# A hybrid decoder step: the fifth value products placed ahead of the first transposed outputs

## The reference

```python
x = half_ffn(x, ...)                                  # x + 0.5 * norm(SwiGLU(norm(x)))
z = rms_norm(x, g) @ w_in                             # split into three groups of heads
o_gla = gated linear attention, 4 heads, dk 64, dv 128
o_sb  = stick_breaking(q, concat(past_k, k), concat(past_v, v), bias, ...)
y     = causal depthwise conv(31) -> LayerNorm -> swish, 256 channels
x = x + rms_norm(concat(o_gla, o_sb, y) @ w_out, g)
x = half_ffn(x, ...)
```

```python
z = einsum('bqhd,bkhd->bhqk', q, k) * scale + bias
log_1mb = where(mask, log_sigmoid(-z), 0)
tail = cumsum(log_1mb, reverse) - log_1mb
w = where(mask, exp(log_sigmoid(z) + tail), 0)
o = einsum('bhqk,bkhd->bqhd', w, v)
```

## Time and profile before

| what | value |
|---|---|
| median of 3 runs | 1409.45 us (1408.23, 1409.45, 1413.83) |
| the profiled execution, its time | 1408.98 us |
| its span | 1407.3 us |
| TensorE busy | 1391.1 us, 99% of the span |
| VectorE busy | 899.6 us, 64% |
| ScalarE busy | 734.5 us, 52% |
| GpSimd busy | 182.6 us, 13% |
| the tails of the two mixers | first layer 396 to 446 us, second 1085 to 1137 us |

### The profile page before, as it was taken

How to read it: one execution, slowest core, us unless ns; L and a number is a source line. 1 busy time by engine, 2 the same in 40 slices (tenths; PEclk the granted TensorE clock), 3 DMA queues, 4 the chain that set the end, 5 groups by cost and what they waited for, 6 DMA issues and landing times.

```text
span 1407.3 us, 26950 instructions
## 1 busy us (share of the span) xinstructions
PE 1391.1 (99%) x10551; PEld 1321.4 (94%) x10551; DVE 899.6 (64%) x1508; ACT 734.5 (52%) x1210; POOL 182.6 (13%) x333
## 2 busy tenths in 40 slices
PE   7999999999999999999999999999999999999998
PEld 6999999988878999999999999999888799999998
DVE  5666544669995876663367665346899858756542
ACT  4544434489766554443365444346887665444441
POOL 1020000323262110000000000021433510000000
PEclk9999999999999999999999999999999999999999
DMA  9575455577799595545545555564868895555541
GB/s 247 150 210 150 141 147 153 156 203 230 210 310 265 145 255 150 150 139 152 155 127 149 151 149 144 152 175 141 252 206 242 287 255 154 151 149 149 148 139 50
DMA packets 391554, 249.41 MB, mean 177 GB/s; under 512 B 16513, under 2 KB 379638, under 8 KB 391428
## 3 DMA queue, kind: packets, MB, share of 16 engines
q1 hardware_dynamic: 375602, 204.94, 51.2%
q0 software_dynamic: 15520, 42.62, 9.7%
q10 hardware_dynamic: 306, 0.13, 0.0%
HBM read 242.10 MB, written 5.53 MB: 176 GB/s over the span
## 4 chain that ended last, share of the span: by engine, by line
PE 94%; DVE 2%; ACT 1%; DMA 1%; issue 1%; SPq 0%; POOLq 0%; POOL 0%; DVEq 0%; ACTq 0%
PE bank L596 25%; PE bank L598 24%; PE bank L597 24%; PE bank L862 3%; PE bank L973 2%; PE bank L877 2%; PE bank L632 2%; PE bank L636 2%; PE bank L633 2%; PE bank L1050 1%; DMA raw<-in_ffn_w_gate 1%; PE bank L827 1%; PE bank L954 1%; PE bank L1168 1%; PE bank L1090 1%
## 5 line engine op out<-in xcount | busy, mean ns | idle before, releaser
L1602 DVE TENSOR_TENSOR w_l<-raw,w_h 128x1024 fp32r<-128x1024 f32 (+1 forms) x332 | 395.4, 1196 | 295.4 <-ACT w_h L1224 295.1
L596 PE MATMUL bank<-hh,w_h 128*128 128x320 f32 x1632 | 512.9, 314 | 0.0
L598 PE MATMUL bank<-hh,w_l 128*128 128x320 f32 x1632 | 504.4, 309 | 0.0
L597 PE MATMUL bank<-hl,w_h 128*128 128x320 f32 x1632 | 504.3, 309 | 0.0
L1224 ACT ACTIVATE w_h<-raw 128x1024 fp32r<-128x1024 f32 (+1 forms) x332 | 332.3, 1030 | 141.4 <-DMA raw<-in_ffn_w_down 101.4
L596 PEld LDWEIGHTS bank<-hh,w_h 128*128 128x128 f32 x1632 | 306.4, 188 | 11.8 <-issue 8.6
L597 PEld LDWEIGHTS bank<-hl,w_h 128*128 128x128 f32 x1632 | 306.5, 188 | 0.6
L598 PEld LDWEIGHTS bank<-hh,w_l 128*128 128x128 f32 x1632 | 306.4, 188 | 0.0
L596 PE MATMUL bank<-guh,w_h 128*128 128x320 f32 x704 | 217.7, 309 | 0.0
L598 PE MATMUL bank<-guh,w_l 128*128 128x320 f32 x704 | 217.4, 309 | 0.0
L597 PE MATMUL bank<-gul,w_h 128*128 128x320 f32 x704 | 217.4, 309 | 0.0
(11 more groups left out here) (297 smaller groups left out, 1604.9 us busy)
## 6 DMA issues: line engine op xcount, KB each, us to landing
raw<-in_ffn_w_gate SPq DMA_DIRECT2D x88, 512.0 KB, 4.0
raw<-in_ffn_w_up SPq DMA_DIRECT2D x88, 512.0 KB, 3.9
raw<-in_ffn_w_down SPq DMA_DIRECT2D x64, 448.0 KB, 3.8
raw<-in_w_in SPq DMA_DIRECT2D x44, 512.0 KB, 4.0
raw<-in_ffn_w_down SPq DMA_DIRECT2D x32, 512.0 KB, 4.0
kpg<-in_cache_sb_k SPq DMA_DIRECT2D x112, 128.0 KB, 3.3
kpg<-in_cache_sb_k POOLq DMA_DIRECT2D x112, 128.0 KB, 2.7
raw<-in_w_out SPq DMA_DIRECT2D x16, 512.0 KB, 6.9
```

Source lines behind the costliest of these rows:

```text
L596: pe.matmul(out, w_h[:, slot, k, :], rhs_h[:, k0 + k, :], start=first, stop=False)
L597: pe.matmul(out, w_h[:, slot, k, :], rhs_l[:, k0 + k, :], start=False, stop=False)
L598: last = pe.matmul(out, w_l[:, slot, k, :], rhs_h[:, k0 + k, :], start=False, stop=end)
L1602: V(dve.tensor_tensor(w_l[:, slot, 0:n, :], raw[:, slot, 0:n, :], w_h[:, slot, 0:n, :].bitcast(F32), ALU.subtract), sm["w_lo"])
```

## The change

On TensorE, `turn_weights(4)` moves from behind `gla_outputs((2, 3))` to the place ahead of `values(3)`. `new_values(1)` and `values(4)` move from behind the convolution's means to directly behind `gla_outputs((2, 3))`, and so ahead of `outputs(0)` and of the prompt's products. `outputs(0)` now writes bank 2 instead of bank 7, `place_outputs(0)` reads it there, and for that `new_values(1)` waits for `oq_placed` 1 instead of `so_done` 4, while `state_products(0)`, which writes bank 2, gets a wait for `so_done` 4. On ScalarE, `place_weights(4)` moves from behind `squares((2, 3))` to ahead of the three `Exp` of `pz_w`. Nothing is computed in another way, and the number of instructions that do work is the same.

```diff
                 def new_values(g):
                     if g:
-                        pe.wait_ge(*at("so_done", 4 * g))
+                        pe.wait_ge(*at("oq_placed", 1))
                     else:
                         pe.wait_ge(*at("rect_done", 6))
...
                     pe.wait_ge(*at("oq_placed", g + 1))
                     for p_ in range(2):
-                        last = pe.transpose(bank[7][:, 256 + p_ * P:256 + (p_ + 1) * P], oq[:, p_ * P:(p_ + 1) * P], cst_("ident"))
+                        last = pe.transpose(bank[OQ_BANK[g]][:, 256 + p_ * P:256 + (p_ + 1) * P], oq[:, p_ * P:(p_ + 1) * P], cst_("ident"))
...
+                pe.wait_ge(*at("o_r", 2))
+                turn_weights(4)
                 values(3)
                 pe.wait_ge(*at("o_read", 2))
                 gla_outputs((2, 3))
-                turn_weights(4)
+                new_values(1)
+                values(4)
+                pe.wait_ge(*at("pz_w", 3))
                 outputs(0)
 
-                pe.wait_ge(*at("pz_w", 3))
                 for h in range(H):
...
                     last = pe.matmul(bank[3][:, 0:T], cst_("mean_ch"), yT[:, c, :], start=(c == 0), stop=(c == 1))
                 last.then_inc(sm["conv_mean"], 1)
-                new_values(1)
-                values(4)
                 turn_weights(5)
...
                 pe.wait_ge(*at("knm_ready", 1))
+                pe.wait_ge(*at("so_done", 4))
                 state_products(0)
...
                 exp_ln()
+                place_weights(4)
                 for n in range(3):
                     act.wait_ge(*at("pz_lw", n + 1))
                     A(nsa(ps_z[:, n, :], ps_z[:, n, :], ACT.Exp), sm["pz_w"])
                 hi(U + U_OUT + 2)
                 squares((2, 3))
-                place_weights(4)
                 act.wait_ge(*at("po_prod", 1))
...
-                            src = bank[7][r, 256 + p_ * P:256 + (p_ + 1) * P].rearrange("p (b h q) -> p b h q", h=H, q=DT)[:, :, 2 * p_ + h2, :]
+                            src = bank[OQ_BANK[g]][r, 256 + p_ * P:256 + (p_ + 1) * P].rearrange("p (b h q) -> p b h q", h=H, q=DT)[:, :, 2 * p_ + h2, :]
...
 O_BANK = (6, 4)
+OQ_BANK = (2, 7)
```

## The result

| | before | changed |
|---|---|---|
| median | 1408.86 us (1406.67 to 1413.83, 20 runs) | 1414.3 us (1411.59 to 1415.41, 20 runs) |
| ratio to before | | 1.0037, 95% interval 1.003 to 1.0043 |
| the profiled execution, time and span | 1408.98, 1407.3 us | 1413.33, 1411.7 us |
| TensorE busy | 1391.1 us | 1392.9 us |

What follows compares the result with a forecast made beforehand. The prediction took TensorE, busy for 99% of the span, as the bound: 1408.98 - 1.61 (clock fall saved) - 0.50 (pages) + 2 x 2.2 (standstill) + 1.6 (one clock fall) = 1412.9 us, range 1408.5 to 1416.5.

Steps and rivals of the forecast that it cites:

- Step 1: Early `turn_weights(4)` costs TensorE 0.59 us and saves as much behind; `place_weights(4)`, 0.60 us, fits a ScalarE hole.
- Step 2: `new_values(1)` and `values(4)` directly behind the gla products: no wait, with 0.5 us left for pages in the worst case.
- Rival D: Pages for `values(4)` come late: up to 1 us in each layer, 1412.9 to 1414.9 us; chance 0.05.
- Step 3: Prompt products 2.39 us later delay ScalarE's 5.84 us chain; TensorE stands 2.2 us ahead of `values(5)` in each layer.
- Step 4: TensorE behind `values(5)`: no idle time takes the 2.2 us back; the `conv_d` wait is hidden behind the longer one.
- Step 5: Page queues: pages of `values(7)` no longer queue behind those of `values(6)`, removing 0.50 us of wait in the second layer.
- Step 6: TensorE's clock: second layer's fall behind the gla products probably saved, 1.61 us; one fall over four places costs 1.6 us.
- Rival B: Clock falls behind the standstill in both layers: 1414.5 us, up to 1417.7 with falls behind gla products; chance 0.28.

Runs made afterwards that it cites:

- e3: The changed kernel with `new_values(1)` and `values(4)` put back behind the convolution's means: 1408.22 us, ratio 0.9998.
- e8: The changed kernel itself, run again without any edit beside before: 1414.27 us, ratio 1.0036.
- e1: The changed kernel with `place_weights(5)` on ScalarE moved directly behind `norms((2, 3))`: 1409.71 us, ratio 1.0005.
- e4: The changed kernel with `turn_weights(5)` behind `values(4)`, `place_weights(5)` behind `squares((2, 3))` and the wait for `conv_d` ahead of `values(5)` left out: 1408.49 us, ratio 1.0002.
- e10: The changed kernel with only the first half of `values(4)` moved, the second half staying behind the convolution's means: 1409.64 us, ratio 1.0008.
- e5: The kernel before, order untouched, with four idle ScalarE copies ahead of `place_weights(5)` to hold the sixth weights back: 1412.73 us, ratio 1.0031.
- e7: The kernel before with the four groups of `values(3)` laid between the 8-column products of `gla_outputs((2, 3))`: 1410.88 us, ratio 1.0017.
- e9: e4 with the last two groups of `values(3)` laid between the 8-column products of `gla_outputs((2, 3))`: 1407.94 us, ratio 0.9995.

## Why the prediction was right

**What bounds the kernel** held: TensorE's list, where every microsecond of the difference is found.

**Step 1** (early transposes and copy, free) held: the copy came at 417.77 in the hole, and e3 costs nothing.

**Step 2** (no wait ahead of `new_values(1)` or in `values(4)`) held in the profile of the changed kernel. The margin for pages had been put at 0.5 us in the worst case, and that was too much trust in the longest landing of one profile: in e8 it was overdrawn by 1.40 us. Rival D exists, at a price above the 1 us given to it, but in one stretch of sixteen.

**Step 3** (standstill of 2.2 us in each layer) was the right mechanism, shown by e1, e3, e4 and e10, and it measured 1.98 us. The term that was too large is the length of the chain, 5.84 us: the changed kernel shows 431.59 - 426.01 = 5.58 us. The row of before at 429.55 was not bound by ScalarE alone. TensorE's transposes for it ended only at 428.85 + 0.66 = 429.51, just ahead of it, and the absent bracket had been read as "no gap". With 5.58 us the prediction's own working gives 2.14 - 0.26 = 1.88 us; the other 0.10 are the steps between groups that it had allowed for and the semaphore (0.06 us assumed, 0.11 measured). Its lower bound of 2.1 us was too high.

**Step 4** held: nothing behind gave time back. The wait for `conv_d`, said to end about where TensorE arrives, does so: in e1 the subtraction ended at 432.21, and TensorE had ended the state products at 432.19. The 0.49 us that the bracket puts down to it there are ScalarE's.

**Step 5** held in the profile: `values(7)` of the second layer has no wait for pages. POOL came to its pages at 1127.61 and not behind those of `values(6)` but after standing 4.01 us:

```profile
1120.03 3.57 POOL L508 DMA_DIRECT2D vpg1a<-in_cache_sb_v  x6 [1.14 <-issue]
1127.61 4.77 POOL L508 DMA_DIRECT2D vpg1b<-in_cache_sb_v  x8 [4.01 <-PE bank L973]
```

**Step 6**, the clock, is the term that was mis-sized. The sum had one fall in all; the profile shows two, and the medians want about as many: 1408.86 + 2 x 1.98 = 1412.8, to which 1.5 us are missing, or 2.0 if the 0.50 us of pages are gone from most runs as from the profile. By the mean clock the changed kernel has (0.9985 - 0.9968) x 1412 us = 2.4 us more of withheld clock than before in the group of e8; part of it falls on standing or behind the last product, where it costs nothing. Rival B, the falls behind the standstill, was the nearer one: e5 shows that holding the weights back in the old order brings the same drop of the mean clock. The counts say it more firmly than the means: a clock below 0.998 had none of the 77 runs of before and none of the 55 of e1, e3, e4, e7 and e9, in which the sixth weights are at most 0.55 us late, but 15 of 20 of the changed kernel, 4 of 6 in e8 and 8 of 10 in e5. The profiles agree: two or three falls each in the six with weights late by 1.5 us or more, none or one in the other seven. What the prediction hoped for, that the new order would save the fall behind the gla products, is not there: e3, e4 and e1 have before's mean clock, with the values behind these products or not. What may act on it is where the 8-column products lie (e7, e9).

That the forecast came within 1.4 us is in part luck. The standstills were put 2 x 0.22 = 0.44 us too high and the clock one fall, some 1.6 us, too low, and the two errors offset in part.

The rule of the Trainium skill, page "TensorE: Matmul & The Clock Gate", section "Why this matters for your kernels", which warns of gaps between bursts of matmuls, was given 1414.5 us in the prediction, and the changed kernel measured 1414.3. That is no proof of the rule: the gaps of which the page's row speaks are longer than the standstills here, so it doesn't foretell these falls. What the runs show goes beyond it in two ways. Weights late by 1.55 us in before's order already took the mean clock from 0.9985 to 0.9970, and every profile in which the clock fell behind the gla products had TensorE busy throughout.

**What stays open.** Whether filling the standstill keeps the clock is not settled. No fall lies behind a filled standstill in six stretches, four lie behind one of 1.5 us or more in six unfilled ones. But the mean clocks of the filled kernels (0.9972, 0.9980, 0.9975) lie between before's and the unfilled ones', 10 of their 21 runs are below 0.998 (27 of 36 of the unfilled), and their profiles have their falls behind the gla products instead, in the first layer too, where the program up to that point is the same as without filling. One profile for each kernel can't say where the falls of the other runs lay.

## What to carry to other kernels

When work on a saturated engine is moved ahead of a product whose result another engine waits for, compare the amount moved with the slack at the far end of that other engine's list, here 2.39 us against 0.31: the wait is about the difference (2.08; measured 1.98), and one early entry in the other list (e1, e4) can remove it. Before a chain is taken to be gapless, look whether an input of its last step was ready in time, as an unmarked wait of 0.2 us hides in a timeline. Lay the releaser that a bracket names beside its own row, too: in e1 it had ended 0.53 us before the wait did. And an input that comes 1.5 to 2 us late to TensorE in mid-run can cost more than the wait itself, here by 1.3 to 1.5 us (with an error of 0.6 to 0.9) for two of them in the mean; for two of 0.84 us the mean showed no such cost.

## What the runs showed of the hardware

The clock isn't the same in two executions of one kernel: of 77 runs of before 20 had 0.999 or 1.0 over the span, the rest 0.998, and their times differ by 1.5 to 2 us in the mean (1405.95 to 1408.65 against 1407.47 to 1411.11). It fell with TensorE busy throughout, behind products with few columns (before's second layer, clock 0.56), and with these spread among wider ones the mean clock was 0.9992 against 0.9985 (e7) and 0.9991 against 0.9982 (e9), though e9's profile still has a fall there. It also fell behind standstills of 1.55 us (both in e5's profile) and 1.98 us (one of two in each profile of the changed kernel). Products of different tile shapes in turn took longer than the same ones apart: by 0.70 us for eight pieces, 0.47 for five.
